# Pooling sums on GpSimd alone, means on VectorE between pair 0's factors; FoX's first stack beside the gate products

## The chip, the cores and the metric

One core of one Trainium2 chip runs the whole program in one launch. The metric is the device time of the launch in microseconds (us), the median of several runs. The engines are TensorE (PE, matmuls), VectorE (DVE), ScalarE (ACT), GpSimd (POOL) and SyncE (SP, which issues the DMAs here). Each works through its own queue in order, and they meet through semaphores.

## The reference, cut to what matters

The input is x of 512 tokens by 1024, in float32. A first block normalises it, projects it with `w_in` and runs three mixers: pooling, gated linear attention (GLA) and forgetting attention (FoX). Their outputs go through `w_o`, then through a feed-forward layer. A second block with two further attentions follows. The change touches only the first block, from the projections to FoX's start. Pooling takes trailing means over 2, 4, 8 and 16 tokens:

```python
def pool_mixer(u, w_pool, pool_scale):
    cs = jnp.cumsum(u32, axis=1)
    for gi, w in enumerate(POOL_WINDOWS):        # 2, 4, 8, 16; 64 channels each
        cnt = jnp.minimum(t1, w)                 # t1 = 1..T
        means.append((cs[:, :, lo:hi] - lagged) / cnt[None, :, None])
    d = (jnp.concatenate(means, axis=-1) - u32)
    y = jnp.einsum('btgc,gcd->btgd', d, w_pool).reshape(B, T, POOL_WIDTH)
    return y * pool_scale
```

GLA works in chunks of 64 tokens: a scan gives bcum, the running sum of the log gates inside a chunk, and then

```python
    q_in, k_in = qh * exp(bcum - ref), kh * exp(ref - bcum)
    o_intra = where(causal, q_in @ k_in.T, 0) @ vh
    kv = (kh * exp(b_last - bcum)).T @ vh        # per chunk
    S = exp(b_last) * S + kv                     # over the chunks
    o = o_intra + (qh * exp(bcum)) @ S_prev      # then RMSNorm, gain, silu(gate)
```

FoX is softmax attention with F_t - F_s added to the logits, F the running sum of log sigmoid of a forget logit.

## The kernel before, in words

Activations lie transposed, channels on the 128 partitions and 512 tokens along them. Each float32 factor of a projection is split into a rounded high half and the rest as low half, and a product of one 128x128 weight tile with 512 tokens is three matmuls (lines 1390, 1392, 1394): high x high, low x high, high x low. Eight such k-tiles fill one PSUM bank: that is a `product`. Products that come out with tokens on the partitions (`product_tok`: the GLA values `gv`, FoX's `fv0`, `fv1`) have four token blocks of 256 columns, each with its own bank (lines 1404 to 1406). All of them share two banks in turn (`d_ring`), so each needs the result before the last to have been taken out of its bank: by VectorE (`scaled`, line 1849) or, for the token blocks, by ScalarE (`out_tok`, line 1606).

Weights come in units of eight tiles. SyncE loads a unit (line 1263) once the low half of the unit three before it is made; ScalarE makes the high half (line 1576), VectorE (line 1827) or GpSimd (line 2175, in four pieces) the low half. Which one does is set by `now["low"]`: VectorE up to `gq1`, GpSimd from `fv0` on. `split` puts unit u+2 into the order when tile 0 of unit u is used.

The order is one list of steps, written when the kernel is built: `do(kind, ...)` adds a step, and each engine's program walks the same list and emits its own part. So the place in the list is the place in every queue. `weave(main, side, per)` (line 119) adds `per` steps of `side` for each `yield` of `main`; a product yields once in two k-tiles, four times in all, a `product_tok` eight times. `go_behind` (line 392) adds steps of waiting generators (`behind`) inside a product, `now["per"]` per pair of k-tiles.

Around the change the list is: the first four products; `gla_front` for both pairs of heads (gate); `pool_means` (GpSimd: for each of four steps two sums, then means and subtractions in halves of 256 tokens; lines 2199, 2206, 2209); the product `gq0` with `gla_scan` of hp=0, `forget` and `gla_scan` of hp=1 inside it; the values `gv`, with `forget_sum` after the first block and pair 0's first four steps (`gla_ref`, `gla_qi`, `gla_ki`, `gla_qe`) from the second on; the step `rows` (three transfers). Then `beside_gla` (`gk1`, `gq1`, GpSimd's fills of the FoX stacks, `fv0`, `fq0`, `fk0`, `fq1`, `fk1`, pooling's product) is woven with `gla_pairs` at 0.8. Then come `stack_fill_late` and the gate products `gg0` and `gg1`, with the steps of `fox_stack(0)` inside them (copies and subtractions that build the operands of FoX's logits, and transfers of rows and of halves between partitions), and then FoX's attention woven with `fox_side` (`fv1` first).

A pair of heads runs through `gla_pair` (line 519): ref, q's factor, k's factor, q's second factor, two attention matmuls with their cuts (lines 1448, 1931, 1934), a transpose (1441), k^T v (1457), the state chain of 14 operations (1945), the output (1466, 1471), its norm (1477).

Each step carries its own waits. One matters here: whatever reuses pooling's places waits for `pool_g("end")`, the last subtraction on GpSimd.

Of the kernel before, what the change touches and what calls it, by code (L numbers as in the profile page):

```python
# [15 lines left out]
T = 512  # L16
NK = D // 128
# [146 lines left out]
def build(nc, wall, xT, vecs, wa, wp, relb, cf, cph, coh, cb, scratch, outT):  # L164
    plan = []
    ctx = ExitStack()
    with ctx:
# [168 lines left out]
        pool_p, pool_a, pool_g = signal("pool_p"), signal("pool_a"), signal("pool_g")  # L336
# [370 lines left out]
        def fox_products(p):  # L707
            yield from product(f"fq{p}", "w_in", 0, cols(O_FQ + 128 * p), "h1", NK,
                               scaled(f"fq{p}", f_st[p][:, 0, :], 0.125, norm=n1, free=[pool_g("end"), gla_v(("S", 0))]))
            yield from product(f"fk{p}", "w_in", 0, cols(O_FK + 128 * p), "h1", NK,  # L710
                               scaled(f"fk{p}", f_st[p][:, 1, :], 1.0, norm=n1, free=[pool_g("end")]))
# [22 lines left out]
        def fox_v(c2):  # L734
            def out(b, tb):
                do("out_tok", name=f"fv{c2}", tb=tb, dst=f_v[:, tb, c2 * 256:c2 * 256 + 256], b=b,
                   scale=rtok[:, tb:tb + 1], norm=norm_a("n1t"), free=[pool_g("end")])
# [13 lines left out]
        do("pool_means")  # L751
        gen = gla_query(0)
        for hp in range(2):
            do("gla_scan", hp=hp, t1=gates[hp][0], t2=gates[hp][1])
            next(gen)
            if hp == 0:
                do("forget")
        run(gen)
        pairs = [gla_pair(hp) for hp in range(2)]
        for n, _ in enumerate(gla_values()):  # L760
            if n == 1:
                do("forget_sum")
            elif n in (3, 4, 5, 6):
                next(pairs[0])
        do("rows")

        def beside_gla():
# [52 lines left out]
        run(gate_products())  # L820
# [544 lines left out]
        def tensor_program(q):  # L1365
# [9 lines left out]
            for kind, s in steps:  # L1375
# [103 lines left out]
                elif kind == "pool_out":  # L1479
                    j = s["j"]  # L1480
                    q.wait_ge(pool_g("end"), s["free"], consts_in())
# [85 lines left out]
        def scalar_program(q):  # L1567
            e = q.e

            for kind, s in steps:  # L1570
# [45 lines left out]
                elif kind == "stack_high":  # L1616
                    i, hl, what, st = s["i"], s["hl"], s["what"], f_st[s["p"]]
                    hd, r = 2 * s["p"] + hl, slice(64 * hl, 64 * hl + 64)
                    q.wait_ge(out_v(f"f{what}{s['p']}"), s["free"], gla_v(("y", 1)))
# [64 lines left out]
                elif kind == "turn":  # L1684
# [5 lines left out]
                    q.wait_ge(turned(s["u"]), s["free_pt"], pool_g("end"), gla_v(("bc", 1)))  # L1690
# [128 lines left out]
        def vector_program(q):  # L1819
            e = q.e  # L1820

            for kind, s in steps:
# [135 lines left out]
                elif kind == "gla_out":  # L1958
# [6 lines left out]
                        *low.tick(("mix", 2 + hp)))  # L1965
# [402 lines left out]
```

## Time and profile before

| what | value |
|---|---|
| median of 3 runs | 1079.06 us (1079.02 to 1080.83) |
| the profiled execution | 1081.06 us |
| its span in the trace | 1079.3 us |
| mean granted clock of TensorE | 0.991 of full speed |
| busy: PE, DVE, ACT, POOL | 1048.5, 585.1, 455.6, 303.9 us |
| GpSimd's products (8) and subtractions (8) for the means | 8.5 and 7.6 us |
| GpSimd's eight sums | 10.1 us |

The span is what the engines' instructions cover; the execution's own time has 1.76 us around it. An engine's busy time says little by itself: what counts is where PE stands idle, and at what clock it runs. "128x512 f32" is partitions by elements; `x4` after a row says that several instructions were merged into it. A time in brackets at a row's end is how long the engine was idle before it, and who released it.

### The profile page before, as it was taken

The numbers are of one execution on the slowest core, as the hardware profiler recorded it, in microseconds if no ns is written. First come the engines' busy times: TensorE is split into PE (matmuls) and PEld (weight loads), VectorE is DVE, ScalarE is ACT, GpSimd is POOL, SyncE is SP. The second block draws the span as 40 slices with busy tenths as digits, with TensorE's granted clock in tenths as the row PEclk, the third lists the DMA queues.
The fourth block names the chain that finished last, engine by engine and source line by source line (L and its number), as shares of the span: only waits on it lengthen the run. The fifth ranks groups of instructions, "written<-read, shape, count | busy, mean of one in ns | idle before, by whom it ended". The sixth has DMA issues, their size and how long they took to land.

```text
span 1079.3 us, 13741 instructions
## 1 busy us (share of the span) xinstructions
PE 1048.5 (97%) x5188; PEld 846.3 (78%) x5188; DVE 585.1 (54%) x1049; ACT 455.6 (42%) x804; POOL 303.9 (28%) x359
## 2 busy tenths in 40 slices
PE   9889999999999999999999998899999999999996
PEld 7768787777888888888888777777787777788885
DVE  6874356656444432454545545798646555325544
ACT  6433446555222311222234466555755554423322
POOL 1745343333010100001014335433433333431100
PEclk9989999999999999999999999999999999999999
DMA  8212133212323233232232326211222333222312
GB/s 283 77 41 79 59 103 96 80 41 97 113 83 107 89 117 98 79 98 98 98 113 83 116 67 206 97 55 64 79 69 84 109 102 108 79 98 79 115 61 78
DMA packets 34801, 102.33 MB, mean 95 GB/s; under 512 B 4560, under 2 KB 8032, under 8 KB 34736
## 3 DMA queue, kind: packets, MB, share of 16 engines
q1 hardware_dynamic: 34736, 101.47, 29.1%
q8 instruction: 41, 0.67, 0.3%
q14 instruction: 24, 0.20, 0.1%
HBM read 93.35 MB, written 4.74 MB: 91 GB/s over the span
## 4 chain that ended last, share of the span: by engine, by line
PE 80%; DVE 9%; ACT 4%; issue 3%; SPq 2%; DMA 1%; POOL 0%; DVEq 0%; ACTq 0%; POOLq 0%
PE bank L1390 22%; PE bank L1394 21%; PE bank L1392 21%; PE bank L1524 3%; PE bank L1515 2%; PE bank L1404 2%; PE bank L1406 1%; PE bank L1405 1%; DVE m L2090 1%; DVE score L2092 1%; PE bank L1496 1%; DVE score L2081 1%; DVE X L2007 1%; DMA X<-xT 1%; DVE acc L1846 1%
## 5 line engine op out<-in xcount | busy, mean ns | idle before, releaser
L1390 PE MATMUL bank<-HH,WH 128*128 128x512 f32 x808 | 328.5, 407 | 7.1 <-ACT g_v L1606 5.4
L1394 PE MATMUL bank<-HH,WL 128*128 128x512 f32 x808 | 316.6, 392 | 0.0
L1392 PE MATMUL bank<-HL,WH 128*128 128x512 f32 x808 | 316.1, 391 | 0.0
L2175 POOL TENSOR_TENSOR WL<-WS,WH 128x256 fp32r<-128x256 f32 x256 | 200.6, 784 | 315.5 <-ACT WH L1576 299.9
L1390 PEld LDWEIGHTS bank<-HH,WH 128*128 128x128 f32 x808 | 153.3, 190 | 43.5 <-ACT g_v L1606 5.6
L1576 ACT ACTIVATE WH<-WS 128x1024 fp32r<-128x1024 f32 x161 | 167.5, 1047 | 41.6 <-PE bank L1394 40.2
L1394 PEld LDWEIGHTS bank<-HH,WL 128*128 128x128 f32 x808 | 152.3, 188 | 33.0
L1392 PEld LDWEIGHTS bank<-HL,WH 128*128 128x128 f32 x808 | 153.0, 189 | 28.9 <-issue 0.7
L1827 DVE TENSOR_TENSOR WL<-WS,WH 128x1024 fp32r<-128x1024 f32 x97 | 125.1, 1295 | 27.1 <-ACT WH L1576 27.0
L2225 POOL TENSOR_TENSOR fa<-fa,fg 128x512 f32<-128x512 f32 x22 | 28.3, 1286 | 271.6 <-DVE fa L2027 271.6
L1394 PE MATMUL bank<-GH,WL 128*128 128x512 f32 x176 | 68.5, 389 | 0.0
L1392 PE MATMUL bank<-GL,WH 128*128 128x512 f32 x176 | 68.5, 389 | 0.0
L1390 PE MATMUL bank<-GH,WH 128*128 128x512 f32 x176 | 68.5, 389 | 0.0
L2007 DVE TENSOR_TENSOR X<-X,bank 128x512 f32<-128x512 f32 x39 | 26.7, 685 | 71.1 <-PE bank L1394 71.0
L1723 ACT ACTIVATE GH<-fa 128x512 fp32r<-128x512 f32 x22 | 13.9, 632 | 114.6 <-POOL fa L2225 114.6
L1404 PE MATMUL bank<-WH,HH 128*128 128x256 f32 x160 | 48.1, 300 | 2.9 <-DVE g_q L1849 2.9
L1588 ACT ACTIVATE sq<-X 128x512 f32<-128x512 f32 x31 | 19.5, 629 | 73.2 <-DVE X L2007 73.1
L1691 ACT ACTIVATE PT<-bank 128x128 f32<-128x128 f32 (+1 forms) x96 | 41.1, 428 | 18.8 <-PE bank L1515 18.6
L1406 PE MATMUL bank<-WH,HL 128*128 128x256 f32 x160 | 45.9, 287 | 0.0
L1405 PE MATMUL bank<-WL,HH 128*128 128x256 f32 x160 | 45.9, 287 | 0.0
L2029 DVE TENSOR_TENSOR GL<-fa,GH 128x512 fp32r<-128x512 f32 x22 | 15.2, 692 | 47.1 <-ACT GH L1723 47.1
L1974 DVE TENSOR_REDUCE small<-bank 128x1 f32<-128x128 f32 (+1 forms) x64 | 30.8, 482 | 16.9 <-PE bank L1497 12.5
(335 smaller groups left out, 1695.3 us busy)
## 6 DMA issues: line engine op xcount, KB each, us to landing
WS<-wall SPq DMA_DIRECT2D x161, 512.0 KB, 3.4
scratch<-rows SPq DMA_DIRECT2D x8, 320.0 KB, 5.0
X<-xT SPq DMA_DIRECT2D x8, 256.0 KB, 6.9
b_t<-scratch SPq DMA_DIRECT2D x8, 256.0 KB, 3.6
outT<-X SPq DMA_DIRECT2D x8, 256.0 KB, 2.1
b_m<-b_m SPq DMA_DIRECT2D x11, 128.0 KB, 2.3
f_s<-f_s SPq DMA_DIRECT2D x8, 128.0 KB
f_m<-f_m SPq DMA_DIRECT2D x8, 128.0 KB
```

The source lines that it names most:

```text
L1390: e.matmul(b[:, :], wh, xh[:, at_k, :], start=k == 0, stop=False)
L1392: e.matmul(b[:, :], wh, xl[:, at_k, :], start=False, stop=False)
L1394: m = e.matmul(b[:, :], wl, xh[:, at_k, :], start=False, stop=k == n - 1)
L1404: e.matmul(b[:, 0:256], xh[:, k, cs], wh, start=k == 0, stop=False)
L1405: e.matmul(b[:, 0:256], xh[:, k, cs], wl, start=False, stop=False)
L1406: m = e.matmul(b[:, 0:256], xl[:, k, cs], wh, start=False, stop=k == NK - 1)
L1524: m = e.matmul(b[64 * hl:64 * hl + 64, 128 * kb:512], v[:, kb, hd * 64:hd * 64 + 64], s["pt"][:, at_pt + 128 * kb:at_pt + 512], start=kb = ...
L1576: e.activation(WH[:, u % NW, :], WS[:, u % NST, :], ACT.Copy).then_inc(*w_hi.tick(u))
L1691: e.activation(dst, s["b"][:, 0:128 * i + 128].rearrange("p (a n) -> p a n", n=128), ACT.Copy).then_inc(*moved.tick(s["u"]))
L1827: e.tensor_tensor(WL[:, u % NW, :], WS[:, u % NST, :], f32(WH[:, u % NW, :]), ALU.subtract).then_inc(*w_low_v.tick(u))
L2007: e.tensor_tensor(X[:, m, :], X[:, m, :], s["b"][:, :], ALU.add).then_inc(*out_v.tick(s["name"]))
L2175: e.tensor_tensor(WL[:, u % NW, cs], WS[:, u % NST, cs], f32(WH[:, u % NW, cs]), ALU.subtract).then_inc(*tick(w_low_g, u if c == 3 else (u ...
```

## The change

GpSimd's step is now `pool_sums`: the eight sums alone. The new step `pool_mean` on VectorE takes one of the four windows: for tokens 16 on, one operation multiplies the sum by the constant 1/w and subtracts u; for the first 16 tokens, whose counts vary, a product with `icnt` and a subtraction follow. The four are placed after the first four steps of pair 0. Pair 0's steps no longer stand beside the values but with `gla_pairs`, woven at 0.95 beside `gk1`, `gq1` and on. `gla_scan` of hp=1 comes after all of `gq0`. What waited for GpSimd's last subtraction waits for VectorE's. `fox_stack(0)` enters before `gg0`; pooling's product stands between `gg0` and `gg1`; both swishes and the late fill come behind `gg1`. ScalarE's first stack copies wait for the matmuls of pair 1's output, no longer for its norm.

```diff
-        def gla_pairs(first, second):
+        def gla_pairs():
+            first, second = gla_pair(0), gla_pair(1)
+            for step in range(4):
+                next(first)
+                do("pool_mean", step=step)
+                yield
+                if step < 3:
+                    yield
             for _ in range(3):
                 next(first)
                 yield
...
-        def gate_products():
-            for j in range(2):
-                yield from product(f"gg{j}", "w_in", 0, cols(O_GG + 128 * j), "h1", NK,
-                                   scaled(f"gg{j}", g_g[:, j, :], 0.5, norm=n1))
-                swish(f"gg{j}", g_g[:, j, :])
+        def gate_product(j):
+            yield from product(f"gg{j}", "w_in", 0, cols(O_GG + 128 * j), "h1", NK,
+                               scaled(f"gg{j}", g_g[:, j, :], 0.5, norm=n1))
...
-        do("pool_means")
+        do("pool_sums")
         gen = gla_query(0)
-        for hp in range(2):
-            do("gla_scan", hp=hp, t1=gates[hp][0], t2=gates[hp][1])
-            next(gen)
-            if hp == 0:
-                do("forget")
+        do("gla_scan", hp=0, t1=gates[0][0], t2=gates[0][1])
+        next(gen)
+        do("forget")
         run(gen)
-        pairs = [gla_pair(hp) for hp in range(2)]
+        do("gla_scan", hp=1, t1=gates[1][0], t2=gates[1][1])
         for n, _ in enumerate(gla_values()):
             if n == 1:
                 do("forget_sum")
-            elif n in (3, 4, 5, 6):
-                next(pairs[0])
         do("rows")
...
             yield from fox_products(1)
-            yield from pool_out()
-
-        weave(beside_gla(), gla_pairs(*pairs), 0.8)
-        do("stack_fill_late")
+
+        weave(beside_gla(), gla_pairs(), 0.95)
         now["per"] = 1.0
         behind.append(fox_stack(0))
+        run(gate_product(0))
+        run(pool_out())
+        run(gate_product(1))
+        for j in range(2):
+            swish(f"gg{j}", g_g[:, j, :])
+        do("stack_fill_late")
...
-        run(gate_products())
...
                 elif kind == "stack_high":
...
-                    q.wait_ge(out_v(f"f{what}{s['p']}"), s["free"], gla_v(("y", 1)))
+                    q.wait_ge(out_v(f"f{what}{s['p']}"), s["free"], gla_p(("y", 1)))
...
+                elif kind == "pool_mean":
+                    step = s["step"]
+                    j, r, total = step // 2, slice(64 * (step % 2), 64 * (step % 2) + 64), p_a[step % 2]
+                    q.wait_ge(pool_g(("sum", step)), consts_in())
+                    e.scalar_tensor_tensor(p_d[r, j, 16:T], total[r, j, 32:16 + T], 0.5 ** (step + 1), p_u[r, j, 32:16 + T],
+                                           ALU.mult, ALU.subtract).then_inc(*pool_v.tick(("rest", step)))
+                    e.tensor_tensor(p_d[r, j, 0:16], total[r, j, 16:32], icnt[r, j, 0:16], ALU.mult).then_inc(
+                        *pool_v.tick(("mean", step)))
+                    q.wait_ge(pool_v(("mean", step)))
+                    e.tensor_tensor(p_d[r, j, 0:16], p_d[r, j, 0:16], p_u[r, j, 16:32], ALU.subtract).then_inc(
+                        *pool_v.tick(("sub", step), *(["end"] if step == 3 else [])))
...
-                        for c in range(2):
-                            cs, cu = slice(256 * c, 256 * c + 256), slice(16 + 256 * c, 272 + 256 * c)
-                            q.wait_ge(before[0], pool_g(("sum", step, c)), consts_in())
-                            e.tensor_tensor(p_d[r, j, cs], dst[r, j, cu], icnt[r, j, cs], ALU.mult).then_inc(
-                                *tick(pool_g, ("mean", step, c)))
-                            q.wait_ge(before[0], pool_g(("mean", step, c)))
-                            e.tensor_tensor(p_d[r, j, cs], p_d[r, j, cs], p_u[r, j, cu], ALU.subtract).then_inc(
-                                *tick(pool_g, ("sub", step) if c else ("sub0", step), *(["end"] if (step, c) == (3, 1) else [])))
```

In `out_tok` of `fv0` and `fv1`, in `fox_products`, in pooling's matmul, in the fills and in the copy after `turn`, `pool_g("end")` becomes `pool_v("end")`.

## Rows read from the trace of the kernel before

**Rows 1.** The page, part 1: busy time, share and instructions.

```profile
PE 1048.5 (97%) x5188; PEld 846.3 (78%) x5188; DVE 585.1 (54%) x1049; ACT 455.6 (42%) x804; POOL 303.9 (28%) x359
```

**Rows 2.** Waits of PE, whole span: for whom, us in total, times, longest.

```profile
PE bank L1390 <- ACT g_v L1606: 5.4, 1, 5.4
PE bank L1404 <- DVE g_q L1849: 2.9, 1, 2.9
...
PE bank L1491 <- DMA f_m<-f_m: 1.8, 1, 1.8
```

**Rows 3.** Windows: us, PE busy (instructions), granted clock, DMA share, GB/s.

```profile
41.90:44.90 3.00, 0.13 (x2) 1.00 0.34 137
59.20:64.20 5.00, 4.98 (x12) 0.54 0.00 0
137.80:142.80 5.00, 5.00 (x31) 0.66 0.40 136
```

**Rows 4.** Timeline of PE: start, us, line, operation, tiles, idle before, releaser.

```profile
44.91 0.38 PE L1404 MATMUL bank<-WH,HH 128*128 128x256 f32 x1 [2.88 <-DVE g_q L1849]
...
59.22 0.79 PE L1390 MATMUL bank<-HH,WH 128*128 128x512 f32 x1 [5.42 <-ACT g_v L1606]
...
64.26 0.68 PE L1448 MATMUL bank<-g_qi,g_ki 64*64 64x64 f32 x16
...
70.49 1.71 PE L1457 MATMUL bank<-g_v,g_kt 64*128 64x128 f32 x16
...
73.61 0.39 PE L1390 MATMUL bank<-HH,WH 128*128 128x512 f32 x1
...
76.33 0.28 PE L1404 MATMUL bank<-WH,HH 128*128 128x256 f32 x1
```

**Rows 5.** Timeline of VectorE, 40 to 77 us.

```profile
41.48 1.12 DVE L1891 TENSOR_TENSOR sq<-sq,tmp 128x512 f32<-128x512 f32 x1
...
44.19 0.66 DVE L1849 SCALAR_TENSOR_TENSOR g_q<-bank,Rb 128x512 f32<-128x512 f32 x1
...
55.11 1.10 DVE L1899 TENSOR_TENSOR tmp<-g_bc 128x512 f32<-128x512 f32 x1
...
60.77 0.69 DVE L1914 TENSOR_TENSOR g_qe<-g_q,g_e 128x512 f32<-128x512 f32 x1 [0.70 <-ACT g_e L1643]
...
64.08 1.22 DVE L1827 TENSOR_TENSOR WL<-WS,WH 128x1024 fp32r<-128x1024 f32 x1 [2.01 <-ACT WH L1576]
65.22 0.41 DVE L1931 TENSOR_TENSOR g_at<-bank,gmask 64x256 f32<-64x256 f32 x1
...
71.92 4.42 DVE L1945 SCALAR_TENSOR_TENSOR g_S<-g_S,g_e,bank 64x64 f32<-64x64 f32 x14
```

**Rows 6.** Timeline of ScalarE, the copy of the third block of `gv`.

```profile
58.71 0.46 ACT L1606 ACTIVATE g_v<-bank,rtok 128x256 f32<-128x256 f32 x1
```

**Rows 7.** Timeline of GpSimd, 31 to 67 us.

```profile
31.52 2.16 POOL L2199 TENSOR_TENSOR p_a<-p_u 128x512 f32<-128x512 f32 x2 [27.29 <-DVE p_u L1849]
...
37.35 3.82 POOL L2199 TENSOR_TENSOR p_a<-p_a 128x512 f32<-128x512 f32 x2
...
59.59 0.52 POOL L2181 MEMSET f_s<- 64x512 f32 x1
...
65.94 0.52 POOL L2187 MEMSET f_m<- 6x512 f32 x1
```

**Rows 8.** Timeline of all engines, 123 to 132.5 us.

```profile
123.16 1.88 PE L1482 MATMUL bank<-p_d,wp_sb 128*128 128x512 f32 x4
...
124.47 0.79 PE L1390 MATMUL bank<-HH,WH 128*128 128x512 f32 x1
...
126.71 1.05 ACT L1576 ACTIVATE WH<-WS 128x1024 fp32r<-128x1024 f32 x1
...
127.90 3.52 POOL L2175 TENSOR_TENSOR WL<-WS,WH 128x256 fp32r<-128x256 f32 x4 [3.44 <-ACT WH L1576]
...
131.90 0.73 SPq L1295 DMA_DIRECT2D f_s<-f_rows  x1
```

More of the change, by code:

```diff
@@ L708, in fox_products @@
             yield from product(f"fq{p}", "w_in", 0, cols(O_FQ + 128 * p), "h1", NK,
-                               scaled(f"fq{p}", f_st[p][:, 0, :], 0.125, norm=n1, free=[pool_g("end"), gla_v(("S", 0))]))
+                               scaled(f"fq{p}", f_st[p][:, 0, :], 0.125, norm=n1, free=[pool_v("end"), gla_v(("S", 0))]))
             yield from product(f"fk{p}", "w_in", 0, cols(O_FK + 128 * p), "h1", NK,
-                               scaled(f"fk{p}", f_st[p][:, 1, :], 1.0, norm=n1, free=[pool_g("end")]))
+                               scaled(f"fk{p}", f_st[p][:, 1, :], 1.0, norm=n1, free=[pool_v("end")]))
         def fox_stack(p):
@@ L736, in out @@
                 do("out_tok", name=f"fv{c2}", tb=tb, dst=f_v[:, tb, c2 * 256:c2 * 256 + 256], b=b,
-                   scale=rtok[:, tb:tb + 1], norm=norm_a("n1t"), free=[pool_g("end")])
+                   scale=rtok[:, tb:tb + 1], norm=norm_a("n1t"), free=[pool_v("end")])
                 return out_a((f"fv{c2}", tb))
@@ L1480, in tensor_program @@
                     j = s["j"]
-                    q.wait_ge(pool_g("end"), s["free"], consts_in())
+                    q.wait_ge(pool_v("end"), s["free"], consts_in())
                     e.matmul(s["b"][:, :], wp_sb[:, j, :], p_d[:, j, :], start=True, stop=True).then_inc(
@@ L1689, in scalar_program @@
                         dst = strided(pt, turned_at(1, i) + 128 * i, 768, i + 1)
-                    q.wait_ge(turned(s["u"]), s["free_pt"], pool_g("end"), gla_v(("bc", 1)))
+                    q.wait_ge(turned(s["u"]), s["free_pt"], pool_v("end"), gla_v(("bc", 1)))
                     e.activation(dst, s["b"][:, 0:128 * i + 128].rearrange("p (a n) -> p a n", n=128),
@@ L2179, in gpsimd_program @@
                         o = 64 - 64 * hl
-                        q.wait_ge(before[0], gla_p(("y", 1)) if (i, hl) == (1, 1) else pool_g("end"))
+                        q.wait_ge(before[0], gla_p(("y", 1)) if (i, hl) == (1, 1) else pool_v("end"))
                         e.memset(f32(f_s2[i][hl][o:o + 64, :]), 0.0).then_inc(*tick(fill, ("zero q", i, hl)))
@@ L2197, in gpsimd_program @@
                             cs, back = slice(16 + 256 * c, 272 + 256 * c), slice(16 + 256 * c - w, 272 + 256 * c - w)
-                            q.wait_ge(before[0], out_v("pu1"), pool_g(("sub", step - 1)) if step else pool_g(("zero", 2)))
+                            q.wait_ge(before[0], out_v("pu1"), pool_g(("sum", step - 1)) if step else pool_g(("zero", 2)))
                             e.tensor_tensor(dst[:, own, cs], src[:, own, cs], src[:, own, back], ALU.add).then_inc(
-                                *tick(pool_g, ("sum", step, c)))
+                                *tick(pool_g, ("sum", step) if c else ("sum0", step)))
                         w *= 2
-                        j, r = step // 2, slice(64 * (step % 2), 64 * (step % 2) + 64)
-                        for c in range(2):
-                            cs, cu = slice(256 * c, 256 * c + 256), slice(16 + 256 * c, 272 + 256 * c)
-                            q.wait_ge(before[0], pool_g(("sum", step, c)), consts_in())
-                            e.tensor_tensor(p_d[r, j, cs], dst[r, j, cu], icnt[r, j, cs], ALU.mult).then_inc(
-                                *tick(pool_g, ("mean", step, c)))
-                            q.wait_ge(before[0], pool_g(("mean", step, c)))
-                            e.tensor_tensor(p_d[r, j, cs], p_d[r, j, cs], p_u[r, j, cu], ALU.subtract).then_inc(
-                                *tick(pool_g, ("sub", step) if c else ("sub0", step), *(["end"] if (step, c) == (3, 1) else [])))
                         src = dst
```

4 lines of the change are left out of this document (2 added, 2 removed).

## The prediction

> **What bounds the kernel now.** I read PE's share on the page first, then who PE waits for, then the granted clock around those waits, and last the timelines of the other engines there. PE is busy 97% of the span [rows 1], so a change elsewhere counts only by what it does to PE's gaps and to PE's clock. Three of PE's longest waits lie inside the changed stretch: 5.4 us for ScalarE's copy of `g_v`, 2.9 us for VectorE's `g_q`, 1.8 us for a transfer into `f_m` [rows 2]. The windows show that two of them cost more than themselves: the 5 us after the 5.4 us wait ran at a mean granted clock of 0.54, those after the 1.8 us wait at 0.66 (the lower of the two levels, 1.2 GHz, and then 2.4 GHz again), while the 2.9 us wait was passed at 1.00 [rows 3]. At full rate the first stretch would have been 5 x 0.46 = 2.3 us shorter, the second 5 x 0.34 = 1.7 us. So 2.9 + 5.4 + 1.8 + 2.3 + 1.7 = 14.1 us is all that there is to win here.
>
> Why each wait is there. (a) `gv`'s second token block takes the PSUM bank of `gq0`. VectorE, done with forget's minimum, goes first to hp=1's subtraction and scan (41.48 to 44.2); only then comes `g_q` [rows 5], and PE restarts at 44.91 [rows 4]. (b) `gk1` takes the bank of `gv`'s third block. ScalarE's copy of it stands behind pair 0's exponentials, whose operand VectorE makes only at 55.11, behind forget's sums [rows 5]; the copy starts at 58.71 [rows 6], PE at 59.22 [rows 4]. (c) The first FoX logits wait for the stack's transfers. SyncE issues the row transfers from 131.90, once GpSimd's low half begun at 127.90 is done; that one waited for ScalarE's split at 126.71, which is queued behind the pooling products' copies, whose matmul PE began at 123.16 [rows 8].
>
> **The scan moved behind gq0.** Nothing is added. VectorE now does `g_q` at 41.48 in place of the subtraction, 0.7 us, so PE restarts at 42.2 instead of 44.91: 2.7 us won. Below, GpSimd's sums still run beside it, as now, so I assume no more. The cost of the scan (2.8 us) goes behind: then two weight halves of 1.2 us each [rows 5], ready by 47.5, and forget's sums, by 53 at most. `gv` ends at 42.2 + 8.9 (44.91 to 53.8 now [rows 4]) = 51.1, so `gk1`'s weights (the first of the two halves) are there in time.
>
> **Pair 0's steps moved behind the values.** ScalarE now meets `gv`'s copies with nothing ahead of them, so each follows its block and the 5.4 us wait goes; with it the low clock, 2.3 us. PE runs through: `gk1` 51.1 to 56.5 (8 k-tiles of 0.68 us, four of them from 73.61 to 76.33 [rows 4]), `gq1` to 62.0, then `fv0` in half blocks of 1.48 us (8.9 / 6). With the rate 0.95, the first attention matmuls of pair 0 come after `fv0`'s first half block (63.4), the transpose after the third (about 67.6 with 2 x 0.6 for the attention matmuls [rows 4]), k^T v after the fourth.
>
> **The means on VectorE.** GpSimd loses 16 instructions, VectorE gains 12: four of 64x496, four products and four subtractions of 64x16. The trace has none of them. Large ones: 0.69 us as a 128x512 one alone, up to 1.12 us as one beside GpSimd. Small ones: above zero and at most 0.32 us, the step of the 14 in the state chain (4.42 us for 14). I take 0.7 + 2 x 0.2 = 1.1 us per step, 4.4 in all, for GpSimd is idle then; the ends are 0.7 and 1.8 per step [rows 5]. Of these the last three stand on a chain that PE meets: `gk1` scaled by 57.2; q's product and mean 1 to 59.0; ScalarE's exponential and split and VectorE's half to 60.8; k's product and mean 2 to 62.6; `gq1` scaled 63.3; two more and mean 3 to 65.8; four cuts at 0.41 to 0.45 to 67.6; k's last product to 68.3. The transpose is due at 67.6. That is a new wait of about 0.8 us, between 0 (0.7 per mean) and 3 us (1.8 per mean). Queued behind it on PE are `fv0`'s other blocks; VectorE's own queue behind holds only the cuts.
>
> GpSimd's cover: two sums of step 0 take 2.16 us, those of step 1 3.82 beside VectorE, the half-wide ones of steps 2 and 3 at most as much; without the means it is done by 42 [rows 7], long before mean 0 at about 54. The fills now wait for mean 3: 65.8 plus 12 memsets in 6.9 us (59.59 to 66.46 [rows 7]) is 72.7, plus `fq0`'s low half of 3.5 us [rows 8] is 76.2. PE reaches `fq0` at 62.0 + 8 x 1.48 + 1.2 + 1.7 [rows 4] + 0.4 for the transpose (an estimate: together as many columns as one matmul of 512) + 0.8 = 77.9. Covered by under 2 us: nothing counted. The scan chain of pair 0 (4.4 us) has four half blocks and two k-pairs of time, the one of pair 1 four k-pairs (5.4 us), so neither shows. SyncE loads weights as before, and its three row transfers come earlier with forget's sums.
>
> The Trainium skill, SBUF — State Buffer, section "SBUF: two separate sides", says that a VectorE operation with two SBUF inputs is shut out for the whole length of a GpSimd operation that reads SBUF, and only of such a one. Of the two readings, memsets in or out, it takes out: by it the fills (now beside VectorE's cuts) cost the chain nothing; were they in, a wait of up to 0.52 us before each of five operations would make it 2.6 us longer. The trace agrees with the page: the cut at 65.22 took 0.41 us among the memsets that end at 66.46 [rows 5, 7].
>
> **FoX's stack beside the gate products.** The order becomes `gg0`, pooling, `gg1`. ScalarE's split for `fv1`'s first half no longer waits for pooling's matmul, so it falls before `gg0` starts instead of 2.2 us after it (126.71 against 124.47), and SyncE's transfers behind it come 2.2 us or more earlier in relation to `gg0`; pooling's matmul between the two products gives them 1.3 us more (123.16 to 124.47) [rows 8]. That is 3.5 us against a wait of 1.8: it goes, and 1.7 us of clock with it. What is late next: the split of the second half is now the one behind pooling's copies. Pooling's matmul to ScalarE's split is 3.6 us (123.16 to 126.71), then 1.05, 0.1 and GpSimd's 3.5 [rows 8]: 8.3 us, and PE wants it 1.3 + 5.4 + 0.3 for the logits (an estimate) + 1.5 = 8.5 after pooling's matmul starts. There is no margin, and I count 0.2 us. Both tanh move behind `gg1` and so ahead of the first row maximum; PE has `fv1`'s blocks to do meanwhile. The late fill, 4 memsets of 0.57 us, moves behind that half on GpSimd, ahead only of halves that PE needs after all of `fv1`.
>
> **The sum.** 2.7 + 5.4 + 2.3 + 1.8 + 1.7 = 13.9 won, 0.8 + 0.2 lost: 12.9 us. The profiled execution took 1081.06 us (1.76 outside its span); the shown runs have a median of 1079.06, 2.0 below it. 1081.06 - 12.9 - 2.0 = 1066.2 us.
>
> **The rivals.**
> 1. VectorE's chain takes the place of the wait (12%). For: it is in order, and pair 0's steps now stand behind results that wait for PE. Against: GpSimd is idle beside it. With means of 1.8 us PE waits 3 us at the transpose and runs some 5 us at 0.54 to 0.66 after it: 2.2 + 2.0 us more lost than forecast, 1070.4 us.
> 2. The wait before FoX moves from the transfer to the weight half (12%). For: the margin is 0.2 us. If GpSimd's half or the copies are 2 us later, PE waits 2 us and the clock falls as it did: 1.8 + 1.7 more lost, 1069.7 us.
> 3. `g_q` is no earlier (5%): if ScalarE's or VectorE's queue holds something I overlook, 2.7 us stay: 1068.9 us. That is also the case in which the first edit does not do what it says.
> 4. Slower (5%): the fills as a gate. Mean 3 now releases GpSimd's fills and, behind them, every FoX weight half. From 67.5 on, each us of mean 3 is a us of PE at `fq0`. With mean 3 ending at 81.5 PE waits 14 us there and loses 2.3 by the clock: 13.9 - 1 - 16.3 = 3.4 slower, 1082.5 us. It decides only if VectorE's chain is 16 us longer than the 14.7 worked out (51.1 to 65.8); twelve contended operations at 1.12 would add 5.
> The clock is a rival's price too: the trace has a 2.9 us wait without a fall and a 1.8 us wait with one [rows 2, 3], so a short new wait may cost 1.7 us or nothing. The Trainium skill, TensorE: Matmul & The Clock Gate, Part 1, holds that the slow rate is the default and activity lifts it; by that, a stretch with no gaps stays fast and the sum stands, and the 2.9 us wait at 1.00 shows that a gap alone does not decide.
>
> **How the numbers follow.** Forecast 66%, rivals 12, 12, 5 and 5. The likeliest one's own range is 1065 to 1068. Below, all 14.1 us and no new wait give 1064.9; above, rivals 1 and 2 reach 1070.4, both in part together 1071.5. Range 1064.5 to 1071.5. A difference of 0.2% (2.2 us) is about what a measurement of this kernel tells from none. Faster takes forecast and rivals 1 to 3 less what I may have missed in the later stages: 0.92; slower 0.05; same 0.03.
>
> **What would show it.** Right: `gv` without a gap before its second block; `gk1` starting about 51; a granted clock of 1.00 from 50 to 130; a wait of up to 1 us at the transpose in `fv0`; GpSimd's sums done by 42 and its fills from about 66; the first logits at about 126 (51.1 + 0.8 + what lies between 59.22 and 137.8 - 1.8 now [rows 3, 4], less 2.3) without a wait. Wrong: a wait of several us in `fv0` or at `fq0`, a half clock after it, or a wait for `WL` at `fv1`'s second half.

## The result, and the profile after

| | before | after |
|---|---|---|
| median beside each other | 1079.04 us (1078.77 to 1080.83) | 1067.57 us (1067.42 to 1068.03) |
| ratio | | 0.9881 [0.9869, 0.9892] |
| profiled execution | 1081.06 us | 1067.55 us |
| span, mean granted clock | 1079.3 us, 0.991 | 1065.7 us, 0.997 |

The change makes the kernel 1.2% faster. The prediction was 1066.2 us, so it is 1.4 us low. From one profiled execution to the other 13.5 us went, where the sum says 12.9. In a later hour before's median was 1080.4 us (15 runs) and the changed kernel's 1067.83, 12.6 apart.

The page of the changed kernel, part 1 (busy time, share, instructions), to be set against [rows 1]:

```profile
PE 1042.7 (98%) x5188; PEld 842.4 (79%) x5188; DVE 582.5 (55%) x1061; ACT 455.8 (43%) x804; POOL 288.4 (27%) x343
```

PE has the same 5188 matmuls and is busy 5.8 us less; the windows below show where. VectorE has 12 instructions more and is yet busy 2.6 us less.

What PE waits for in the changed kernel (for whom, us in total, times, longest):

```profile
PE bank L1420 <- DVE zb L1853: 2.8, 1, 2.8
PE bank L1427 <- POOL acc L2226: 2.4, 1, 2.4
PE bank L1567 <- ACT sq L1813: 2.1, 1, 2.1
PE bank L1394 <- DVE a_q L2132: 1.6, 2, 1.3
PE bank L1394 <- DVE HL L1841: 1.1, 1, 1.1
```

All three rows of [rows 2] are gone, and none of the five left lies between `gv` and FoX. To see where the time went I cut both traces at the same pieces of work: the start of `gv`, the first FoX logits, the column sums of the second and of the third norm. Before, in windows (stretch: length, PE busy (instructions), granted clock, DMA share, GB/s):

```profile
38.74:137.78 99.04, 88.92 (x562) 0.97 0.22 69
...
142.78:255.62 112.84, 111.07 (x615) 1.00 0.26 77
255.62:619.48 363.86, 363.08 (x1599) 1.00 0.30 99
619.48:1079.30 459.82, 443.30 (x2227) 0.99 0.29 92
```

And after:

```profile
39.48:125.36 85.88, 85.88 (x561) 1.00 0.25 80
125.36:130.36 5.00, 5.00 (x44) 1.00 0.42 129
130.36:242.41 112.05, 109.93 (x603) 1.00 0.26 77
242.41:606.26 363.85, 363.07 (x1599) 1.00 0.30 99
606.26:1065.70 459.44, 441.68 (x2227) 0.99 0.28 92
```

From `gv` to the first logits 99.04 - 85.88 = 13.16 us went: 10.1 of waits (99.04 - 88.92) and 3.0 of busy time. Of the 3.0, 2.4 lie behind the start of `gk1`, where before had its low clock. The other 0.65 lie in `gv`, at a granted clock of 1.00 both times: PE was busy there for 12.17 us before and for 11.52 after. They are the ends and restarts at the two gaps that are gone (a matmul before a gap counts 0.28 us where starts are otherwise 0.12 apart), and 0.26 us around a matmul that started late at 40.33, right behind a low half that VectorE finished at 40.28.

PE now has no gap at all in this stretch. From the logits to the second norm it is 0.8 us (5.00 + 112.84 against 5.00 + 112.05; the window of five us is the last row of [rows 3]), to the third nothing, to the end 0.4. Before `gv`, 0.74 us is lost: `gv` starts at 39.48 instead of 38.74, by a wait of 1.1 us for `HL` in the first loads, a stretch that the change doesn't touch. The sum is 13.6 of span.

In the last stretch PE is busy 1.6 us less (443.30 to 441.68) and gains almost nothing by it. Before, the five us behind the wait for `acc` ran at a mean clock of 0.66, and PE waited 1.2 us for `zb` next. Changed, they ran at 1.00, and the wait for `zb` is 2.8.

Where PE stands in the changed kernel (timeline: start, us, line, operation):

```profile
51.00 0.40 PE L1394 MATMUL bank<-HH,WH 128*128 128x512 f32 x1
...
61.90 0.28 PE L1408 MATMUL bank<-WH,HH 128*128 128x256 f32 x1
...
67.82 0.60 PE L1445 MATMUL bank<-ident,g_kh 128*128 128x128 f32 x4
...
77.27 0.43 PE L1394 MATMUL bank<-HH,WH 128*128 128x512 f32 x1
```

No brackets stand behind these rows: `gk1`, `fv0`, the transpose and `fq0` start with no idle time before them.

### The profile page after: what moved, and what is told of

Its sections match the earlier page's. It is cut to its first block, busy times and chain, and to the rows that moved or that the text cites. A ratio compares the mean times of both kernels' runs of the same rounds, so it can differ in the third digit from the quotient of the medians.

```text
span 1065.7 us, 13737 instructions
## 1 busy us (share of the span) xinstructions
PE 1042.7 (98%) x5188; PEld 842.4 (79%) x5188; DVE 582.5 (55%) x1061; ACT 455.8 (43%) x804; POOL 288.4 (27%) x343
## 3 DMA queue, kind: packets, MB, share of 16 engines
HBM read 93.35 MB, written 4.74 MB: 92 GB/s over the span
## 4 chain that ended last, share of the span: by engine, by line
PE 84%; DVE 8%; ACT 4%; issue 2%; DMA 1%; SPq 0%; DVEq 0%; ACTq 0%
PE bank L1394 23%; PE bank L1398 22%; PE bank L1396 22%; PE bank L1528 3%; PE bank L1519 2%; PE bank L1408 2%; DVE m L2105 1%; PE bank L1410 1%; PE bank L1409 1%; DVE score L2107 1%; PE bank L1500 1%; DVE score L2096 1%; DMA X<-xT 1%; DVE X L2022 1%; ACT WH L1580 1%
## 5 line engine op out<-in xcount | busy, mean ns | idle before, releaser
L1723 ACT ACTIVATE fs<-fg 128x512 f32<-128x512 f32 x22 | 13.9, 632 | 59.3 <-DVE fg L2033 59.3
```

## The experiments

All medians with 95% intervals of the ratio to the kernel before, which ran beside them at 1080.3 to 1080.9 us. In prose, "changed" is the changed kernel.

**The changed kernel in the later hour** (no edit).

> The changed kernel unaltered, on the chip and in the hour of the three below, to compare them with, and for the granted clock of its runs and of the kernel before. Theory: the gain in the profiled executions (13.5 us) is larger than the one of the medians (11.5 us) because the profiled execution of before ran part of its time at half clock where the others do not; then here too the difference of medians is 11 to 12 us, and the 1.7 us of clock after the third wait is the term that is sometimes absent. Rival: that the two first medians happened to lie apart by chance; then the difference of medians is 13 us or more.

Measured: 1067.83 us (1067.16 to 1068.2), 0.9884 [0.9871, 0.9898]. The medians lie 12.6 us apart, between what the two explanations asked for, so this decides for neither. It is the figure that the others are set against. `gv` starts at 38.39 in its trace and not at 39.48, without the wait for `HL`.

**The scan alone.** The kernel before, with only hp=1's scan moved behind `gq0`:

```diff
-        for hp in range(2):
-            do("gla_scan", hp=hp, t1=gates[hp][0], t2=gates[hp][1])
-            next(gen)
-            if hp == 0:
-                do("forget")
+        do("gla_scan", hp=0, t1=gates[0][0], t2=gates[0][1])
+        next(gen)
+        do("forget")
         run(gen)
+        do("gla_scan", hp=1, t1=gates[1][0], t2=gates[1][1])
```

> The kernel before with hp=1's scan moved behind gq0 and nothing else. Theory (a): the 2.9 us wait for g_q goes to about 0.2. But gv's fourth block does not end the wait behind it: that one (for ScalarE's copy of gv) is set by VectorE's queue, which has the same work in front of pair 0's first step, so it grows by what is won here: PE's gap before gk1 becomes 8.1 us and the time stays within 0.5 us of before. Rival, as the sum of the prediction treats it: the terms add, and it is 2.7 us faster than before.

Measured: 1080.44 us, 1.0002 [0.9993, 1.0011]: nothing. Its waits on PE:

```profile
PE bank L1389 <- ACT g_v L1605: 8.1, 1, 8.1
...
PE bank L1490 <- DMA f_m<-f_m: 1.8, 1, 1.8
```

The 2.9 us wait for `g_q` shrank to 0.2, and all of it came back some 14 us later: the wait for `g_v` was 5.4 and is 8.1. PE arrived earlier at a gate that opens when VectorE's chain is done, and that chain had not become shorter. The five us behind the 8.1 ran at 0.50. The wait for `f_m` was passed at 1.00 here, which is why this trace's span is 1.2 us shorter than before's while the medians are the same.

**The steps of pair 0 alone.** The kernel before, with pair 0's steps woven into what follows the values:

```diff
-        def gla_pairs(first, second):
+        def gla_pairs():
+            first, second = gla_pair(0), gla_pair(1)
+            for step in range(4):
+                next(first)
+                yield
+                if step < 3:
+                    yield
...
-            elif n in (3, 4, 5, 6):
-                next(pairs[0])
...
-        weave(beside_gla(), gla_pairs(*pairs), 0.8)
+        weave(beside_gla(), gla_pairs(), 0.95)
```

> The kernel before with pair 0's steps moved behind the values (woven at 0.95) and nothing else: the scan of hp=1 still ahead of g_q, the means on GpSimd, pooling before gg0. Theory: each wait is set by what stands ahead of its releaser. The wait for g_q stays at 2.9 us; the wait for ScalarE's copy, 5.4 us, goes with the 2.3 us of clock behind it: 7.5 us faster than before, and together with the scan moved 10.2, so that the scan's 2.7 us are won only once this is done (alone it won nothing). Rival: with the means still on GpSimd and the scan ahead of g_q, VectorE is late for the attention matmuls in fv0 and a new wait of 2 us or more takes part of it: 5 us or less.

Measured: 1073.37 us (1071.77 to 1075.01), 0.9931 [0.9918, 0.9943], 7.3 us faster. Its waits:

```profile
PE bank L1407 <- DVE g_q L1852: 2.9, 1, 2.9
...
PE bank L1494 <- DMA f_m<-f_m: 1.8, 1, 1.8
```

So the 5.4 us wait goes with this edit alone, and the low clock behind it. The 7.3 us look like these two (5.4 + 2.3 = 7.7), but the trace holds more. The wait for `g_q`, passed at 1.00 before, is followed by the low clock here (a row of the timeline, then two windows):

```profile
44.41 0.58 PE L1407 MATMUL bank<-WH,HH 128*128 128x256 f32 x1 [2.88 <-DVE g_q L1852]
```

```profile
44.41:49.41 5.00, 5.00 (x23) 0.50 0.50 144
49.41:54.41 5.00, 5.00 (x41) 0.92 0.21 75
```

That costs 5 x 0.50 + 5 x 0.08 = 2.9 us. The wait for `f_m` was passed at 1.00, which saves 1.7. Together 5.4 + 2.3 + 1.7 - 2.9 = 6.5, and the span is 6.6 us shorter than before's. The five runs lie from 1071.77 to 1075.01, so which of these prices is paid may differ from run to run; only one run has a trace. The scan's 2.7 us can be won only on top of this edit, and no run has just the two.

**The steps put back beside the values.** Changed, with pair 0's steps beside `gv` again; the scan, the means' engine and FoX's order stay:

```diff
-            first, second = gla_pair(0), gla_pair(1)
+            first, second = pair0, gla_pair(1)
             for step in range(4):
-                next(first)
                 do("pool_mean", step=step)
...
+        pair0 = gla_pair(0)
         for n, _ in enumerate(gla_values()):
             if n == 1:
                 do("forget_sum")
+            elif n in (3, 4, 5, 6):
+                next(pair0)
```

> The changed kernel with pair 0's first four steps beside the values again, as before, the means still on VectorE behind the values and the scan behind gq0. Theory (b): ScalarE's copy of gv's third block is again behind exponentials that wait for forget's sums on VectorE. These now end at 51 (GpSimd idle beside them), so the copy comes at about 54 and PE waits 54.5 - 50.8 = 3.7 us instead of 8.1; with the clock behind it 5 to 6.5 us slower than the changed kernel. Rival: forget's sums end so much earlier with GpSimd idle that the steps' place no longer matters: within 1 us of the changed kernel.

Measured: 1072.41 us (1071.78 to 1073.8), 0.9922 [0.9905, 0.9938], 4.6 us more than changed. The wait is back, and so is the low clock behind it; here its row, and then the window behind it:

```profile
PE bank L1396 <- ACT g_v L1612: 2.7, 1, 2.7
```

```profile
53.00:58.00 5.00, 5.00 (x16) 0.66 0.00 0
```

2.7 + 5 x 0.34 = 4.4 us, less than expected (a wait of 3.7 us, 5 to 6.5 in all). The wait is 2.7 here and 8.1 with the scan alone; in between lies what GpSimd no longer does beside VectorE, and the next two runs part that out.

**The means alone.** The order of before, with the sums on GpSimd and the four means on VectorE behind the values:

```diff
-        do("pool_means")
+        do("pool_sums")
...
+        for step in range(4):
+            do("pool_mean", step=step)
         do("rows")
```

> The kernel before with the means on VectorE, placed after the values, GpSimd making the sums alone; the rest of the order as before. Theory: in this order GpSimd's reads do cost, for forget's sums (7.4 us beside them, 4.7 alone, as the changed kernel shows) stand ahead of what ScalarE's copy of gv waits for: the wait for g_q shrinks to about 2.4, the one for the copy from 5.4 to 2.7 to 3 us, with 1.7 to 2.3 us of clock left: 2.5 to 4 us faster than before. Rival: the means cost nothing in one place and win nothing in the other: within 1 us of before.

Measured: 1076.82 us (1074.83 to 1078.47), 0.9962 [0.995, 0.9975], 3.85 faster. Its waits:

```profile
PE bank L1443 <- DVE g_kh L1924: 2.4, 1, 2.4
...
PE bank L1406 <- DVE g_q L1851: 1.7, 1, 1.7
```

The wait for `g_q` is 1.7 instead of 2.9 and that for `g_v` 1.3 instead of 5.4: VectorE's chain is shorter without GpSimd's means beside it. A new one of 2.4 us came at pair 0's transpose, behind the means. The expected 2.5 to 4 us are met by other waits than the expected ones (2.4 and 2.7 to 3, with the clock's loss). None of these three waits was followed by a low clock, but the 1.8 us for `f_m` was, at 0.66.

**The means back on GpSimd.** Changed, with GpSimd's products and subtractions as before, no `pool_mean`, and every wait for `pool_v("end")` turned back to `pool_g("end")`; all order stays:

```diff
-                do("pool_mean", step=step)
...
-        do("pool_sums")
+        do("pool_means")
```

> The changed kernel with the means and subtractions back on GpSimd (pair 0's steps still behind the values, the scan behind gq0, FoX's stack as changed). Theory: the new order alone won the time, and the means only had to be somewhere; GpSimd has them done by 60 us, before fv0 needs them, and its reads beside VectorE lengthen VectorE's operations there from 0.7 to 1.1 us, which costs the restart after gq0 (41.5 instead of 41.2) at most 0.5 us; forget's sums end at 55 instead of 51, so ref comes at 56, and the chain to k's factor still makes it by about 67: within 1 us of the changed kernel, either side. Rival: moving the means is what counts; the slowed VectorE makes PE wait in fv0 for the attention matmul or the transpose: 2 to 5 us slower than the changed kernel, with a half clock behind the wait.

Measured: 1067.67 us (1067.53 to 1068.96), 0.9886 [0.9872, 0.9899]: the time of the changed kernel as far as the medians tell. Its timeline of VectorE, the first and the last operation of forget's sums:

```profile
47.80 0.98 DVE L1867 TENSOR_TENSOR fw<-fw,fw 8x512 f32<-8x512 f32 x1
...
54.36 0.84 DVE L1872 CAST part<-F 8x512 fp32r<-8x512 f32 x1
```

and the same two in the changed kernel:

```profile
46.00 0.68 DVE L1867 TENSOR_TENSOR fw<-fw,fw 8x512 f32<-8x512 f32 x1
...
50.30 0.42 DVE L1872 CAST part<-F 8x512 fp32r<-8x512 f32 x1
```

VectorE is slower beside GpSimd and 4.5 us later at the end of it (55.2 against 50.7), and PE has no wait behind it: `gk1` starts at 50.99, `fv0` at 61.9, `fq0` at 77.45. In the new order what PE needs from behind forget's sums, pair 0's factors, comes in time. Small costs remain in the trace. `gv` started at 38.77 and took 12.22 us against 11.52, with a wait of 0.2 for `g_q` and the late start that before had at 40.33. From `gv` to the second norm it is 203.8 us against 202.9 in the changed kernel. The changed kernel's own trace hides this in the times above, since its `gv` started 0.7 us later.

**The means twice.** Changed, with each mean's three operations done twice (these lines stand ahead of the three of `pool_mean`):

```diff
+                    e.scalar_tensor_tensor(p_d[r, j, 16:T], total[r, j, 32:16 + T], 0.5 ** (step + 1), p_u[r, j, 32:16 + T],
+                                           ALU.mult, ALU.subtract).then_inc(*pool_v.tick(("rest1", step)))
+                    e.tensor_tensor(p_d[r, j, 0:16], total[r, j, 16:32], icnt[r, j, 0:16], ALU.mult).then_inc(
+                        *pool_v.tick(("mean1", step)))
+                    q.wait_ge(pool_v(("mean1", step)))
+                    e.tensor_tensor(p_d[r, j, 0:16], p_d[r, j, 0:16], p_u[r, j, 16:32], ALU.subtract).then_inc(
+                        *pool_v.tick(("sub1", step)))
+                    q.wait_ge(pool_v(("sub1", step)))
```

> The changed kernel with each mean computed twice on VectorE (12 more operations, about 1 us per step). It prices rival 1. Theory: VectorE's chain to k's last product (done 67.63) has 0.2 us of slack against the transpose (67.82); gk1's wait swallows the first mean, so 3 x 0.95 = 2.9 us arrive there, less 0.2: PE waits 2.7 us at the transpose. The clock is the open point: if a wait of that length costs what the 1.8 us wait cost, 4 to 4.5 us slower than the changed kernel; if it passes as the 2.9 us wait did, 2.7 us. Rival: the later means are absorbed by VectorE's pauses for ScalarE (0.65 us before the weight half), 2 us or less.

Measured: 1070.63 us (1069.34 to 1071.6), 0.9903 [0.9888, 0.9917], 2.8 us more than changed. Its wait and the window behind it:

```profile
PE bank L1445 <- DVE g_kh L1926: 2.1, 1, 2.1
```

```profile
70.20:75.20 5.00, 5.00 (x32) 0.66 0.00 0
```

k's last product ended at 70.07 instead of 67.63: of the 3.0 us that three doubled means add, 2.4 reach the chain, and PE waits for 2.1 of these. So the chain stands 0.2 us ahead of the transpose, without a wait. From `gv` to the second norm the trace is 3.8 us longer (206.7 against 202.9), which is wait and clock, 2.1 + 1.7; the median moved by 2.8.

**The fills made long.** Changed, with five memsets more in each of the three early stacks, 15 in all:

```diff
                         q.wait_ge(before[0])
+                        e.memset(f32(f_m2[i][hl][o:o + 6, :]), 1.0).then_inc(*tick(fill, ("stack0", i, hl)))
+                        for n in range(4 if kind == "stack_fill" else 0):
+                            q.wait_ge(before[0])
+                            e.memset(f32(f_m2[i][hl][o:o + 6, :]), 1.0).then_inc(*tick(fill, ("again", i, hl, n)))
+                        q.wait_ge(before[0])
```

> The changed kernel with 5 more memsets in each of the three early fills (15 more, 0.58 us each: 8.7 us on GpSimd, ahead of FoX's first weight halves). It prices the gate of rival 4. Theory: fq0's low half, now ready at about 75.9, comes at 84.6, and PE reaches fq0 at 77.3: a wait of 7.3 us for WL there, 2 to 2.5 us of clock behind it, and some of GpSimd's later halves late too: 9 to 11 us slower than the changed kernel. Rival: GpSimd has enough slack over the next units (3.2 us of work in 5.5) that only the first wait shows, and the clock stays: 7 us.

Measured: 1076.33 us (1075.82 to 1077.03), 0.9956 [0.9942, 0.9971], 8.5 us more. Its wait and the window behind it:

```profile
PE bank L1394 <- POOL WL L2190: 6.6, 1, 6.6
```

```profile
83.00:88.00 5.00, 4.94 (x16) 0.62 0.49 159
```

6.6 + 5 x 0.38 = 8.5 us, a little under the expected 7.3 and 9 to 11. The gate of rival 4 is real and has its price, wait plus clock; the changed kernel only stays on the right side of it. From the first memset to the first half behind them it is 15.6 us here and 6.95 in the changed kernel, so the fills are 8.6 us longer (a memset comes every 0.575 us), and `fq0` is 6.8 us late. The fill adds one memset to the late stack too, which nothing waits for.

**Pooling's product first.** Changed, with pooling's product ahead of `gg0`:

```diff
-        run(gate_product(0))
         run(pool_out())
+        run(gate_product(0))
         run(gate_product(1))
```

> The changed kernel with pooling's product before gg0 instead of between gg0 and gg1; nothing else. Theory (c): ScalarE's split is again behind pooling's copies, SyncE's row transfers come after it, and PE waits about 1.8 us for the transfer into f_m before FoX's first logits, with up to 1.7 us of clock after it: 1.8 to 3.5 us slower than the changed kernel. Rival: the wait is gone for another reason (both swishes behind gg1, or ScalarE's stack copies no longer waiting for VectorE): then the same as the changed kernel within 0.5 us.

Measured: 1069.08 us (1067.51 to 1069.82), 0.9894 [0.9881, 0.9908], 1.25 us more than changed, under the expected 1.8 to 3.5; the intervals overlap. In the profile the step is plain: the wait and the low clock come back, and SyncE issues the row transfers later.

```profile
PE bank L1495 <- DMA f_m<-f_m: 1.8, 1, 1.8
```

```profile
126.50:131.50 5.00, 5.00 (x32) 0.66 0.38 125
```

```profile
120.38 0.73 SPq L1299 DMA_DIRECT2D f_s<-f_rows  x1
```

In the changed kernel that last row is this one, 3.8 us earlier:

```profile
116.60 0.73 SPq L1299 DMA_DIRECT2D f_s<-f_rows  x1
```

Wait and clock make 1.8 + 1.7 = 3.5. From `gv` to the second norm the trace is 2.8 us longer (205.7 against 202.9), so part is given back behind the logits, as above in the comparison of the traces. The median says 1.25; where the rest went I don't know.

**Two trials at what is left.** The third norm's sums of squares on VectorE instead of GpSimd:

```diff
-                add_square(("n3", m), total_g, X[:, m, :], None, out_v(("down", m, 1)))
+                add_square(("n3", m), total_v, X[:, m, :], None, out_v(("down", m, 1)))
...
-            ready = [total_g(("n3", 7)), total_g(("n3f", 7))]
+            ready = [total_v(("n3", 7)), total_g(("n3f", 7))]
```

> The changed kernel with the eight additions of squares for the third norm (n3) on VectorE, GpSimd keeping those of n3f. Theory: PE's longest wait left, 2.4 to 3.0 us for GpSimd's acc at the end of the feed-forward part, is two additions of 1.29 us after the last square; with one each on two engines it is 1 to 1.3 us shorter: 1 us faster than the changed kernel. Rival: ScalarE's two squares and VectorE's X and HL set that wait and the addition on VectorE delays the low half: no faster.

Measured: 1067.69 us (1066.27 to 1068.62), 0.9875 [0.986, 0.989]. A miss: I had put the wait for `acc` down to the third norm, and the line is a helper's. The timeline of the changed kernel shows where it is, at the column sums of a later latent:

```profile
606.26 1.88 PE L1427 MATMUL bank<-acc,ones 128*128 128x512 f32 x4
...
661.04 1.13 PE L1427 MATMUL bank<-acc,ones 128*128 128x512 f32 x2 [2.44 <-POOL acc L2226]
```

Changed, with those sums one pair of k-tiles later; the first of the two runs also set a mark one step earlier by which a later attention's products may begin, the second moved the sums alone:

```diff
             for n, _ in enumerate(z_products("za", P_ZA, 0)):
-                if n == 2:
+                if n == 3:
                     i, b = column_sums("lq", acc[0], total_g(("lq", 2)))
...
-                if n == 4:
+                if n == 3:
                     dsa_in[p] = True
```

> The changed kernel with the column sums of the query latent one pair of k-tiles later in the product za0. PE's longest wait left (2.4 to 3.0 us for GpSimd's acc, L1427) stands there, not at the third norm, as the run with the n3 sums on VectorE showed. Theory: 1.5 us of products fill that much of the wait, ScalarE's norm of it comes as early as before: 1 to 1.5 us faster than the changed kernel. Rival: the next wait of the part (1.2 or 2.8 us for VectorE, before the MLA values) takes it over: no faster.

Measured: 1066.95 us (1065.47 to 1067.7), 0.9868 [0.9853, 0.9883], the wait 1.4 instead of 2.4 us, and 0.9 us less than changed where 1 to 1.5 were expected.

> The run before it in this series (column sums of the query latent one k-pair later) also set the mark that lets the third attention's products begin one step earlier. Here only the column sums move. Theory: the wait for acc (2.4 to 3.0 us in the changed kernel) falls to about 1.4 and the time is within 1 us of the changed kernel, 1066.5 to 1067.8 us; the mark does nothing. Rival: the 0.9 us by which the earlier run's median stood lower came from the mark, and this one is at 1067.8 or above.

Measured: 1067.83 us (1067.06 to 1069.0), 0.9884 [0.9867, 0.99], with the wait at 1.5 us. In both the next wait, for `zb`, is 2.8 us as in the changed kernel's first trace, and the five us behind it ran at 0.66 and 0.65 where that trace had 1.00. One us off a wait can't be told from nothing here, and whether the first run's 0.9 us is the mark or scatter stays open; no version beats the changed kernel by what these runs can show.

## Why the prediction was right, and where it was off

The mechanisms and the direction held, and the time lies in the range. The steps:

| step | predicted | measured |
|---|---|---|
| `gk1` starts | 51.1 | 51.00 |
| `fv0` starts | 62.0 | 61.90 |
| a mean on VectorE | 1.1 us | 0.66 + 0.16 + 0.17 = 1.0 |
| k's last product done | 68.3 | 67.63 |
| wait at the transpose | 0.8 us | none (67.82) |
| GpSimd's sums done | 42 | 41.73 |
| fills done | 72.7 | 72.09 |
| `fq0` starts | 77.9 | 77.27 |
| first logits | 126 | 125.36, clock 1.00 |
| `fv1`'s second half | 0.2 us lost | no wait |
| profiled to profiled | -12.9 | -13.5 |

**The terms.** The 10.1 us of waits all went (9.9 were counted), and both clock terms had their size. From the start of `gk1` to the logits PE's busy time fell by 2.4, where I had 2.3. The first logits and what PE did up to the next ones took 4.74 us before and 3.17 after, 1.6 less, where I had 1.7. Around these right terms stand five that the sum doesn't have:

| not in the sum | us |
|---|---|
| busy time in `gv` | +0.65 |
| the two losses of 1.0, which did not come | +1.0 |
| the last stretch | +0.4 |
| given back between the second logits and the second norm (113.10 to 113.88) | -0.8 |
| the start of `gv`, later by the wait for `HL` | -0.74 |

They come to 0.5 together, so that 12.9 and the 13.6 of span lie so near each other is partly luck. Of the 0.8 given back, half is idle time and half busy time; what holds PE there I did not find.

**The mean.** These are the three operations of mean 0 in the changed kernel (timeline of VectorE):

```profile
54.40 0.66 DVE L1974 SCALAR_TENSOR_TENSOR p_d<-p_a,p_u 64x496 f32<-64x496 f32 x1
54.98 0.16 DVE L1976 TENSOR_TENSOR p_d<-p_a,icnt 64x16 f32<-64x16 f32 x1
55.18 0.17 DVE L1979 TENSOR_TENSOR p_d<-p_d,p_u 64x16 f32<-64x16 f32 x1
```

The size was taken from the nearest rows, 0.7 + 2 x 0.2, and it measured 1.0; GpSimd is idle there.

**What failed is the step to the median.** The sum subtracts 2.0 us because the profiled execution of before took 1081.06 and the three runs shown 1079.06. Later medians of the same kernel are 1080.3 to 1080.9 (38 runs, 1078.0 to 1082.5), so the profiled run was an ordinary one and the three were low. With nothing subtracted the sum gives 1068.2 against 1067.57 and 1067.83. The four runs with a mean clock of 0.993 took 1078.0 to 1078.7, the other 34, at 0.989 to 0.992, 1078.9 to 1082.5. The changed kernel's in the later hour lie within 1.0 us (1067.16 to 1068.2) at 0.995 to 0.997. That the missing scatter is that of the clock behind the gaps fits these numbers; it was not tested by itself. (The range's remark that all 14.1 us give 1064.9 should say 1065.0.)

**The terms were not each worth their number.** The prediction adds 2.7 for the scan to 5.4 for the steps as if either could be had alone. The runs show otherwise: scan alone 0, steps alone 7.3, both with the rest 12.6. Rival 3's price ("2.7 us stay") can hold only with the steps moved, and it leaves out the clock: in the trace of the steps alone that wait cost 2.9 us more than itself. The sum's own reading of it, a wait that is passed at 1.00, came from one trace. Two gates in one in-order queue count as their last one, until that one is gone.

**The means.** The prediction has no gain for them and a loss of 0.8. In the new order moving them is worth nothing that the medians show (1067.67 against 1067.83) and 0.9 us between two traces, in the old one 3.85 us. So the title's first half is not what made the kernel faster: the order did, and it takes away the place where GpSimd's company hurt.

**The rivals.** 1: no wait at the transpose; the doubled means priced it at 2.1 + 1.7 in the trace and 2.8 us in the median, where the rival says 4.2 more for 3 us of wait. 2: the second weight half came in time: GpSimd makes it from 122.91 to 126.85, and the first matmul of the k-tile that needs it starts at 127.09. So the margin is 0.2 us, as the prediction had it, and no wait of PE for `WL` shows. 3: `g_q` came at once:

```profile
41.17 0.69 DVE L1853 SCALAR_TENSOR_TENSOR g_q<-bank,Rb 128x512 f32<-128x512 f32 x1
```

4: the gate stands where the rival put it. Fills longer by 8.6 us made `fq0` 6.8 us late, so the changed kernel has 1.8 us of slack there (the prediction: under 2). Its own trace agrees: the half is done at 75.4, `fq0` starts at 77.27.

## What to carry to other kernels

When several waits lie on one in-order path, take the edits that free the last gate first, and price the earlier ones only together with it: an earlier start in front of a closed gate is worth nothing. Work on an engine beside the bottleneck is worth moving only as long as something that the bottleneck needs stands behind it; ask that again after each reordering, since here the same move was worth 3.85 us in the median and then nothing. And take the difference between a profiled run and the median from many runs or leave it out.

## What the runs showed of the hardware

**VectorE beside GpSimd.** Forget's operations on 8x512 took 0.98 and 0.84 us beside GpSimd's reads and 0.68 and 0.42 without them, and the 128x512 ones 1.10 against 0.69 [rows 5]. The one that makes `g_q`, with one input in PSUM, took 0.66 us beside GpSimd's products before (44.19 [rows 5]) and 0.69 after, within 0.03 us of each other. The fills, memsets from 65.22 to 72.09, don't slow VectorE: the product at 66.94 took 0.69 us among them, as alone.

```profile
66.94 0.69 DVE L1926 TENSOR_TENSOR g_kh<-g_k,tmp 128x512 f32<-128x512 f32 x1
```

The Trainium skill, SBUF — State Buffer, section "SBUF: two separate sides", names two kinds of VectorE operation that can be shut out by GpSimd: those in a 2-port perf mode, and those with two SBUF inputs, the latter only against a GpSimd operation that reads SBUF. The trace agrees on the second kind: 0.69 us for two SBUF inputs among memsets, 1.10 beside GpSimd's reads. The casts (0.42 alone, 0.84 beside GpSimd) have a single SBUF input; whether they are the first kind no run shows. The prediction's row for the memsets, the cut at 65.22, doesn't test this, since one of its inputs is in PSUM. The one at 60.77 [rows 5] does: two SBUF inputs, a memset that began at 60.74 beside it, and 0.69 us.

**A short gap may or may not cost clock.** The mean granted clock of the five us behind a wait of PE. At 0.50 all of them ran at the lower level, 1.2 GHz, at 0.66 a part, and at 1.00 none:

| wait, us | clock behind it | in the trace of |
|---|---|---|
| 1.3 and 1.7 | 1.00 | means alone |
| 1.8 (`f_m`) | 0.66 | before, pooling first, means alone |
| 1.8 (`f_m`) | 1.00 | scan alone, steps alone |
| 2.1 | 0.66 | means twice |
| 2.4 | 1.00 | means alone; changed (`acc`) |
| 2.4 and 2.5 (`acc`) | 0.69 and 0.50 | means twice; pooling first |
| 2.7 | 0.66 | steps beside the values; before (`acc`) |
| 2.9 (`g_q`) | 1.00 | before |
| 2.9 (`g_q`) | 0.50 | steps alone |
| 3.0 (`acc`) | 0.66 | changed, in the later hour |
| 5.4, 6.6, 8.1 | 0.54, 0.62, 0.50 | before, fills long, scan alone |

The 1.8 us wait of the steps alone, for instance:

```profile
132.00:137.00 5.00, 4.99 (x42) 1.00 0.47 136
```

So from 1.8 to 2.9 us the length of the wait doesn't decide it, and a wait of the same length at the same place went both ways in two kernels (`f_m`, `g_q`, `acc`). What decides was not settled here. For a forecast, a gap's price has a part that is sure, itself, and up to 3 us more that may come.

**A low clock may cost nothing.** In the trace of the later hour the changed kernel waits like this:

```profile
PE bank L1427 <- POOL acc L2226: 3.0, 1, 3.0
...
PE bank L1420 <- DVE zb L1853: 1.2, 1, 1.2
```

The first trace had 2.4 and 2.8 us. There the five us behind `acc` ran at 1.00, here at 0.66, which is 1.7 us more of work, and the wait for `zb` is 1.6 us shorter. Both times PE goes on 7.2 us after the matmul behind `acc` (661.04 to 668.25, and 660.94 to 668.14). The next gate is VectorE's, and the time lost to the clock would have been spent waiting there.
